# Store before weights, partial results after five sides, six early rows of h: one transformer layer step on one TensorE-bound core

## The chip, the cores and the metric

The kernel runs on one core of a Trainium2 chip. The metric is device time in microseconds (us) of one execution. The kernel before takes 2395.6 us in the median of three runs (2394.22 to 2397.26). One further execution was profiled; all rows below come from it. In the profile PE is TensorE (PEld its weight loads), DVE is VectorE, ACT is ScalarE, POOL is GpSimd, SP is SyncE; SP, ACT and POOL also issue the transfers (DMA) between the chip's main memory and the on-chip buffers.

## The reference, cut to what matters

One layer of a streaming encoder on 1024 prompt tokens and 32 sample tokens, with D_MODEL = 2048, all in float32:

```python
n = _rmsnorm(h, g_in)
z = n @ w_in                                   # 2048 x 6152: q, k, v, forget gate, ga, u, gs
att = _fox_attention(q, ..., k_all, v_all, ...)
ssm = _s5(u, ...)                              # state space scan, GELU, GLU with w_glu
mixed = concatenate([att * silu(ga), ssm * silu(gs)])
h = h + mixed @ w_out                          # 2048 x 2048
e = _rmsnorm(pe @ w_pe, g_pe)
h = h + e * sigmoid(h @ w_pg)                  # 2048 x 2048
y = _rmsnorm(h, g_final)
```

The two branches, the projections and the last norm are all computed; the keys, values, log forget gates and final states are outputs as well.

## The kernel before, in words

Every float32 product is done as three TensorE matmuls of rounded halves: an operand x is split into a high part (ACT casts it) and a low part (DVE subtracts the high part from x), and hi·hi, hi·lo and lo·hi are summed. The stages follow each other: the front (input projection, with the state-space branch in it), attention, side (the `w_pe` and `w_glu` products), mix (output projection), output (`w_pg` gate and final norm).

**Front and mix** are Strassen-Winograd products. A step p is one pair of column blocks, with seven products r = 0..6 of 24 matmuls each. The contraction is done in two halves: front steps 0 to 23 and mix steps 0 to 7 work on the first half, steps 24 to 47 and 8 to 15 on the second. At the change of halves, the seven stationary activation tiles ("sides", `t_act` and `m_t_act`) are exchanged: POOL reloads side s as soon as the last product that used it is done (`reload_side`), ACT makes its high part (`high_side`), DVE its low part (`low_side`, L1238 and L2890). In the first half a step's result is stored as a partial result (`cT<-zb`: L420 in the front, L2658 in the mix), and in the second half it is fetched back (`zb<-cT`, `load_part`, L667 and L2716) and put into the accumulators by ACT (`seed_x` L977 and L2795, then the second seed L982 and L2800).

SP carries the weights: each step needs two raw weight tiles of 512 KB (`load_w(p, 0)` and `load_w(p, 1)`, L415 and L2649). DVE first adds within them (the sums: L1297, L1301, L1306, L1309; L2918 and so on in the mix), ACT casts (L971, L2790), and DVE makes the low parts (L1316, L2936). DVE also adds products into the results (L1284, L1285, L1323, L1341, L1349; c22 is L1341, in the second half L1343; L2943, L2956, L2958 and L2964 in the mix). In each step the front's SP issues `load_w(p + 1, 1)`, then the store of the partial result, then `load_w(p + 2, 0)`; the mix's SP issues the store first and then both weight tiles.

In step 5 of the front the forget-gate weights are prepared by DVE behind its other work (`split_wf`, L1500 to L1506), and PE multiplies them in step 6 (L773).

**Side to mix.** The last output of the side stage is `mixT<-e_out`, issued by ACT (L2473); ACT ends the stage only when it has landed, and all engines wait for each other at a stage's end.

**Mix to output.** `hT` holds the layer's h in main memory, 16 rows of 128. The output product of a part (part 0: 512 tokens, part 1: 544) runs over w_pg column tiles; each tile needs all 16 rows of h, split. h comes back in groups of two rows through a ring of buffers `h_raw` with 4 groups; the first 4 groups are loaded during the mix, and their first 4 rows split behind the mix's last work (L2837 on ACT, L2976 on DVE), the rest in the output stage (L3206, L3270). At the turn from part 0 to part 1 DVE splits 12 rows of the next part, does the gate of part 0's last tile (L3279, L3284, L3287), splits the last 4 rows and then a weight tile (L140, L145). PE's transposes `y_ps` (L3158) of the gated tile stand inside part 1's first tile.

Within an engine, instructions run in program order, and what an engine needs from another it waits for with semaphores. The program has no scheduler: the loops in the code set the order.

Of the kernel before, what the change touches and what calls it, by code (L numbers as in the profile page):

```python
# [60 lines left out]
RING_H, EARLY_H = 4, 4  # L61
# [139 lines left out]
def stage_front(nc, d, G):  # L201
# [3 lines left out]
    with ExitStack() as ctx:  # L205
# [198 lines left out]
        def _(sp):  # L404
# [131 lines left out]
            for p in range(2 * NP):  # L536
# [88 lines left out]
        def _(pool):  # L625
# [279 lines left out]
        def _(act):  # L905
# [192 lines left out]
            def extra(p, j):  # L1098
# [96 lines left out]
        def _(dve):  # L1195
# [425 lines left out]
            def extra(p, j):  # L1621
# [702 lines left out]
def stage_side(nc, d, G):  # L2324

    with ExitStack() as ctx:
# [27 lines left out]
        gated_done, mix_stored = ([sem(f"{n}{b}") for b in range(2)] for n in ("gated_done", "glu_stored"))  # L2354
# [73 lines left out]
        def _(act):  # L2428
# [140 lines left out]
def stage_mix(nc, d, G):  # L2569


    with ExitStack() as ctx:  # L2572
# [66 lines left out]
        def _(sp):  # L2639
# [15 lines left out]
            for p in range(2 * NPM):  # L2655
# [9 lines left out]
                if p == last:  # L2665
                    for i in range(4):
                        sp.wait_ge(z_put[i], PUT + mix_count(NPM + RING_H - 1))
                    for g in range(RING_H):
# [7 lines left out]
        def _(pool):  # L2676
# [40 lines left out]

            for r in range(NRIDE):
                move_rides(r)
            for s in range(7):  # L2720
                reload_side(s)
                if s == 2:
                    load_part(NPM)
# [49 lines left out]
        def _(act):  # L2773
# [78 lines left out]
            for p in range(2 * NPM):  # L2852
                for j in range(7):
# [16 lines left out]
                    if j == 5 and NPM - 1 <= p < last:  # L2870
                        seed_x(p + 1)
                    high(7 * p + j + RING_W - 1)
                    for s in range(7):
                        if 7 * p + j == 7 * (NPM - 1) + s + 3:
# [3 lines left out]
            for k in range(EARLY_H):  # L2878
                high_h(k)

        @block.vector
        def _(dve):
# [112 lines left out]
            for p in range(2 * NPM):  # L2995
                for j in range(7):
                    if p == 0 and j < 3:
# [5 lines left out]
                    if j == 5:  # L3003
                        c22(p)
                    if j == 6:
# [7 lines left out]
                    for s in range(7):  # L3013
                        if 7 * p + j == 7 * (NPM - 1) + s + 4:
# [10 lines left out]
            for k in range(EARLY_H):  # L3025
                low_h(k)


def stage_output(nc, d, G):
# [11 lines left out]
    RING = 4  # L3041
    with ExitStack() as ctx:
# [6 lines left out]
        side, total, sig, h2 = ([sb(f"{n}{b}", [P, WM]) for b in range(2)]  # L3049
                                for n in ("side", "total", "gate_sig", "h2_"))  # L3050
        junk = nc.alloc_sbuf_tensor_at("junk", [P, YT, P], F32, offset=nc.sbuf_usable_end // 32 * 32 - 4 * YT * P)
# [136 lines left out]
        def _(act):  # L3188
# [12 lines left out]
            def high_h(part, k):  # L3201
                act.wait_ge(h_loaded[k // 2 % RING], 16 * (part * 2 + k // 2 // RING + 1))
# [6 lines left out]
                if k % 2 and (RING if part else RING + EARLY_H // 2) <= g < KD // 2:  # L3209
# [27 lines left out]
            for g in range(RING, RING + EARLY_H // 2):  # L3237
# [28 lines left out]
        def _(dve):  # L3266
# [64 lines left out]
            for part in range(2):  # L3331
# [61 lines left out]
def program(nc, d):  # L3393
# [3 lines left out]
    with ExitStack() as ctx:  # L3397
# [13 lines left out]
                          for i, n in enumerate("qkv")]  # L3411
# [10 lines left out]
                                            offset=(nc.sbuf_base + 31) // 32 * 32 + 256 + (3 + t) * 4 * KQ * HN) for t in range(2)]  # L3422
        G["m_loaded"] = [sem(f"m_w_loaded{s}") for s in range(3)]
        G["m_raw"] = [nc.alloc_sbuf_tensor_at(f"m_raw{s}", [P, KQ, 2 * P], F32, offset=top + s * 8 * KQ * P)
# [5 lines left out]
        def low(name, shape, dt=F32):  # L3430
# [9 lines left out]
                                             offset=top - 4 * RING_H * 2 * (T - 512)),  # L3440
# [27 lines left out]
```

## Time and profile before

| what | value |
|---|---|
| median of three runs | 2395.6 us |
| profiled execution, device time | 2394.27 us |
| its span in the profile | 2392.5 us |
| mean granted TensorE clock | 0.973 of full |
| PE busy | 2205.9 us (92%) |
| DVE busy | 1617.7 us (68%) |
| ACT busy | 906.0 us (38%) |
| POOL busy | 324.2 us (14%) |
| bytes moved | 424.80 MB, mean 178 GB/s |

The profiled execution lies 1.3 us under the median; 1.8 us of it lie outside the span. PE is idle for 186.6 us of the span, in pieces at the stage changes and the changes of halves. Times in the rows are us from the start of the span.

### The profile page before, as it was taken

What the parts mean: (1) busy time and instruction counts of PE and PEld (TensorE: products, weight loads), DVE (VectorE), ACT (ScalarE), POOL (GpSimd) and SP (SyncE); (2) the same over time, 40 slices, a digit from 0 to 9 for tenths busy, and PEclk for the clock granted to TensorE, in tenths of its full rate; (3) what the DMA queues carried; (4) which work ended last, traced back from release to release, by engine and by line L of the source; (5) the groups of instructions that cost most, each with busy time, mean ns of one, the idle gap of its engine ahead of it and who ended that gap; (6) DMA issues with size and microseconds to landing.
All of it is one profiled execution on the core that took longest, in us unless ns stands there. A gap on an engine that the chain in (4) does not pass through costs nothing. (4 is left out here: it accounts for less than half of the span.)

```text
span 2392.5 us, 44144 instructions
## 1 busy us (share of the span) xinstructions
PE 2205.9 (92%) x16355; PEld 2114.8 (88%) x16355; DVE 1617.7 (68%) x2941; ACT 906.0 (38%) x1843; POOL 324.2 (14%) x428
## 2 busy tenths in 40 slices
PE   3999999999899999999789978978989999999995
PEld 3999999999899999999778868978989987888995
DVE  6778766766787887886456646666657666666663
ACT  6542333333533333334366636224343331113112
POOL 0011000000111211111243410001111211111110
PEclk9999999999999999999899989989999999999997
DMA  8484444544757878785376655454556665346332
GB/s 244 146 258 111 142 138 123 151 135 127 272 185 207 230 218 237 217 224 165 129 238 202 199 178 188 130 198 148 189 206 233 217 221 159 111 126 202 100 100 97
DMA packets 362384, 424.80 MB, mean 178 GB/s; under 512 B 76064, under 2 KB 294792, under 8 KB 354336
## 3 DMA queue, kind: packets, MB, share of 16 engines
q1 hardware_dynamic: 306128, 266.62, 37.7%
q0 software_dynamic: 29504, 110.42, 13.5%
q10 hardware_dynamic: 26576, 45.40, 5.9%
q8 instruction: 112, 1.84, 0.3%
q14 instruction: 64, 0.52, 0.1%
HBM read 270.01 MB, written 143.68 MB: 173 GB/s over the span
## 5 line engine op out<-in xcount | busy, mean ns | idle before, releaser
L761 PE MATMUL acc<-t_act,w_hi 128*128 128x264 f32 x5376 | 889.1, 288 | 11.8 <-DVE zb L1323 3.8
L761 PEld LDWEIGHTS acc<-t_act,w_hi 128*128 128x128 f32 x5376 | 749.6, 189 | 18.6 <-issue 17.2
L761 PE MATMUL acc<-t_act,w_lo 128*128 128x264 f32 x2688 | 549.0, 286 | 0.0
L761 PEld LDWEIGHTS acc<-t_act,w_lo 128*128 128x128 f32 x2688 | 418.2, 189 | 0.0
L2763 PE MATMUL m_acc<-m_t_act,m_hi 128*128 128x264 f32 x1792 | 296.4, 288 | 19.9 <-ACT m_acc L2806 9.8
L1316 DVE TENSOR_TENSOR w_lo<-w_raw_f,w_hi 128x512 fp32r<-128x512 f32 x288 | 198.1, 688 | 145.2 <-ACT w_hi L971 144.6
L971 ACT CAST w_hi<-w_raw_f 128x512 fp32r<-128x512 f32 x288 | 177.9, 618 | 269.0 <-PE acc L761 247.4
L2763 PEld LDWEIGHTS m_acc<-m_t_act,m_hi 128*128 128x128 f32 x1792 | 252.9, 191 | 20.7 <-issue 19.7
L3170 PE MATMUL post_acc<-h_hi,w_post_hi 128*128 128x272 f32 (+1 forms) x768 | 211.2, 329 | 7.8 <-PEq L2572 4.3
L3170 PE MATMUL post_acc<-h_hi,w_post_lo 128*128 128x272 f32 (+1 forms) x768 | 208.2, 326 | 0.0
L3170 PE MATMUL post_acc<-h_lo,w_post_hi 128*128 128x272 f32 (+1 forms) x768 | 208.0, 325 | 0.0
L2763 PE MATMUL m_acc<-m_t_act,m_lo 128*128 128x264 f32 x896 | 184.6, 288 | 0.0
L3170 PEld LDWEIGHTS post_acc<-h_hi,w_post_hi 128*128 128x128 f32 x768 | 129.6, 190 | 21.0 <-DVE h_lo L3270 5.2
L2763 PEld LDWEIGHTS m_acc<-m_t_act,m_lo 128*128 128x128 f32 x896 | 141.0, 191 | 0.0
L3170 PEld LDWEIGHTS post_acc<-h_lo,w_post_hi 128*128 128x128 f32 x768 | 129.8, 190 | 10.6
L3170 PEld LDWEIGHTS post_acc<-h_hi,w_post_lo 128*128 128x128 f32 x768 | 129.1, 190 | 11.4
L2936 DVE TENSOR_TENSOR m_lo<-m_raw,m_hi 128x512 fp32r<-128x512 f32 x96 | 66.0, 689 | 53.3 <-ACT m_hi L2790 53.3
L3223 ACT ACTIVATE junk<-y_ps 128x128 f32<-128x128 f32 (+1 forms) x144 | 37.0, 274 | 170.6 <-PE y_ps L3158 170.6
L3284 DVE TENSOR_TENSOR h<-h,gate_sig 128x512 f32<-128x512 f32 (+1 forms) x32 | 22.7, 709 | 106.6 <-ACT gate_sig L3216 106.5
L652 POOL DMA_DIRECT2D zT<-zb x80 | 43.3, 542 | 343.0 <-DVE zb L1332 144.9
L3120 POOL TENSOR_TENSOR total<-h_hi,h_lo 128x512 f32 (+3 forms) x32 | 50.1, 1567 | 288.1 <-DVE h L3287 273.9
L2790 ACT CAST m_hi<-m_raw 128x512 fp32r<-128x512 f32 x96 | 59.2, 620 | 63.8 <-PE m_acc L2763 57.3
(435 smaller groups left out, 3633.9 us busy)
## 6 DMA issues: line engine op xcount, KB each, us to landing
w_raw_f<-in_w_in_dram SPq DMA_DIRECT2D x96, 512.0 KB, 4.1
w_raw<-in_w_pg_dram SPq DMA_DIRECT2D x64, 512.0 KB, 4.7
cT<-zb SPq DMA_DIRECT2D x24, 1056.0 KB, 4.6
zb<-cT POOLq DMA_DIRECT2D x96, 264.0 KB, 5.8
zT<-zb POOLq DMA_DIRECT2D x80, 264.0 KB, 3.7
m_raw<-in_w_out_dram SPq DMA_DIRECT2D x32, 512.0 KB, 5.8
eT<-e_out ACTq DMA_DIRECT2D x16, 528.0 KB, 3.1
cT<-m_zb SPq DMA_DIRECT2D x8, 1056.0 KB, 5.0
```

The source lines that it names most:

```text
L652: pool.dma_start(d["zT"][row:row + P, tok:tok + HN], zb[b][:, i]).then_inc(z_put[i], 16)
L761: mm = pe.matmul(out[:, c, 0:QN], w[:, k, :], t_act[:, SIDE[r], x, k, c * QN:(c + 1) * QN], start=(opens and k == 0 and m == 0), stop=(k = ...
L971: nc.scalar.copy(w_hi[n % RING_W][:], factor(p, r)).then_inc(hi_done, 1)
L1316: TT_(w_lo[n % RING_W][:], factor(n // 7, n % 7), w_hi[n % RING_W][:].bitcast(F32), ALU.subtract) \
L2763: mm = pe.matmul(out[:, c, 0:QN], w[:, k, :], t_act[:, MSIDE[r], x, k, c * QN:(c + 1) * QN], start=(opens and k == 0 and m == 0), stop=(k ...
L2790: nc.scalar.copy(w_hi[n % RING_W][:], factor(p, r)).then_inc(hi_done, 1)
L2936: TT_(w_lo[n % RING_W][:], factor(n // 7, n % 7), w_hi[n % RING_W][:].bitcast(F32), ALU.subtract) \
L3120: nc.gpsimd.tensor_tensor(total[b][:, 0:WIDTH[part]], row(hi, part, m).bitcast(F32), row(lo, part, m).bitcast(F32), ALU.add).then_inc(tota ...
L3170: mm = pe.matmul(acc[b][:, c, 0:width], w[:, k, :], a[:, k, start:start + width], start=(k == 0 and n == 0), stop=(k == KD - 1 and n == 2))
L3223: s = nc.scalar.activation(junk[0:rows, t], tr_ps[b][0:rows, t * P:(t + 1) * P], ACT.Square, accum_out=ssq[0:rows, t, bass.ds(m, 1)])
L3284: nc.vector.tensor_tensor(h2[b][:, 0:w], h2[b][:, 0:w], sig[b][:, 0:w], ALU.mult).then_inc(e_gated, 1)
```

## The change

Six edits, in the order of the program:

1. Front, SP: the store of a step's partial result is issued before `load_w(p + 1, 1)` in place of after it.
2. Front and mix, POOL: the first partial result is fetched back after five sides have been reloaded, in place of three.
3. Front and mix, ACT and DVE: `high_side` and `low_side` come one product slot later.
4. The ring of h has six groups in place of four, all six loaded in the mix. Six rows are split early in place of four, and DVE does this before c12 of the mix's last step. The last two groups are loaded at the start of the output stage.
5. Output, DVE: at the turn to part 1 the weight tile is split before the last four rows, and the gate of part 0's last tile comes after both.
6. Side: ACT no longer waits for the last stores of `mixT`; POOL and DVE wait for them in the mix before they read that data.

```diff
-                load_w(p + 1, 1)
                 if 1 <= p <= NP:
                     store_part(p - 1)
+                load_w(p + 1, 1)
...
             for s in range(7):
                 reload_side(s)
-                if s == 2:
+                if s == 4:
                     load_part(NP)
...
-                    if 7 * p + j == 7 * (NP - 1) + s + 3:
+                    if 7 * p + j == 7 * (NP - 1) + s + 4:
                         act.wait_ge(sides_moved[s], 16 * (RIDES + 1))
                         high_side(7 + s, s, t_act[:, SIDE[s], 1].bitcast(F32))
...
-                    if 7 * p + j == 7 * (NP - 1) + s + 4:
+                    if 7 * p + j == 7 * (NP - 1) + s + 5:
                         low_side(7 + s, s, t_act[:, SIDE[s], 1].bitcast(F32))
...
             for b in range(2):
                 act.wait_ge(e_stored[b], 16 * KD // 2)
-                act.wait_ge(mix_stored[b], 16 * KS // 2)
...
+            for b in range(2):
+                pool.wait_ge(G["glu_stored"][b], 16 * KS // 2)
             for r in range(NRIDE):
                 move_rides(r)
...
-RING_H, EARLY_H = 4, 4
+RING_H, EARLY_H = 6, 6
...
+                    if p == last and j == 6:
+                        for k in range(EARLY_H):
+                            low_h(k)
                     if j == 6:
                         c12(p)
...
             residual(last, 2)
             residual(last, 3)
-            for k in range(EARLY_H):
-                low_h(k)
...
-            for g in range(RING, RING + EARLY_H // 2):
+            for g in range(RING, GROUPS_H):
                 load_h(0, g)
...
                 if part == 0:
                     for k in range(KD - 4):
                         low_h(1, k)
-                gate(part, KD - 1, 1, KD // 2 - 1)
-                if part == 0:
+                    W.split_tile(dve, nc, KD + 1, 1, True)
                     for k in range(KD - 4, KD):
                         low_h(1, k)
-                    W.split_tile(dve, nc, KD + 1, 1, True)
+                gate(part, KD - 1, 1, KD // 2 - 1)
                 fill(part, KD - 1, 1)
```

What moves on the engines. On SP, one step of the front (`w_raw_f` are weights, `cT<-zb` the store, `wf_rawa` the forget-gate weights, so this is step 5):

```order
-L415 DMA w_raw_f<-in_w_in_dram 128x4x256
-L420 DMA cT<-zb 128x2112
-L415 DMA w_raw_f<-in_w_in_dram 128x4x256
+L420 DMA cT<-zb 128x2112
+L415 DMA w_raw_f<-in_w_in_dram 128x4x256 x2
 L487 DMA wf_rawa<-in_w_in_dram 128x16x8
```

The store of 1056 KB now stands ahead of both weight tiles. The same happens in each of the steps 1 to 24.

On DVE, the change of halves in the front, before the change (`t_act` is the low part of a side, `w_lo` of a weight):

```order
 L1488 TENSOR_TENSOR d_diag<-d_bc_93,ident 16x64
 L1491 TENSOR_TENSOR kern<-kern,d_diag 16x4x16
-L1238 TENSOR_TENSOR t_act<-t_act 128x2112
 L1341 TENSOR_TENSOR zb<-zb,acc 128x528
 L1301 TENSOR_TENSOR w_raw_f<-w_raw_f 128x4x128
...
 L1297 TENSOR_TENSOR w_raw_f<-w_raw_f 128x4x128
 L1316 TENSOR_TENSOR w_lo<-w_raw_f,w_hi 128x512
+L1238 TENSOR_TENSOR t_act<-t_act 128x2112
 L1343 TENSOR_TENSOR u_out<-acc,zb 128x66x8
```

The low part of side 0 no longer stands ahead of step 23's c22 (L1341); every side's low part moves one slot back, and that of side 6 now stands ahead of step 24's c22 (L1343).

On POOL, the same place (`t_act<-tS` are sides, `zb<-cT` partial results):

```order
-L641 DMA t_act<-tS 128x2112 x3
-L667 DMA zb<-cT 128x528 x4
-L641 DMA t_act<-tS 128x2112 x4
+L641 DMA t_act<-tS 128x2112 x5
+L667 DMA zb<-cT 128x528 x4
+L641 DMA t_act<-tS 128x2112 x2
```

Two transfers of a side pass the four pieces of the partial result.

## Rows read from the trace of the kernel before

**Rows 1.** The page, section 1: busy time of each engine.

```profile
PE 2205.9 (92%) x16355; PEld 2114.8 (88%) x16355; DVE 1617.7 (68%) x2941; ACT 906.0 (38%) x1843; POOL 324.2 (14%) x428
```

**Rows 2.** Windows (stretch, length, busy us per engine, PEclk, DMA share, GB/s).

```profile
214.00:216.00 2.00, 2.00 (x11) 2.00 (x11) 1.83 (x10) 0.00 (x0) 0.00 (x0) 0.50 0.89 376
```

**Rows 3.** Timeline of SP, step 5 of the front (start, duration, engine, line, operation).

```profile
187.93 0.39 SPq L415 DMA_DIRECT2D w_raw_f<-in_w_in_dram  x1
192.00 0.35 SPq L420 DMA_DIRECT2D cT<-zb  x1
```

**Rows 4.** Timeline of DVE and PE there ([idle before <-releaser]).

```profile
194.26 0.69 DVE L1297 TENSOR_TENSOR w_raw_f<-w_raw_f 128x512 f32<-128x512 f32 x1
...
213.74 5.69 PE L773 MATMUL oth<-t_act,wf_twoa 128*128 128x264 f32 x32 [4.68 <-DVE wf_twoa L1506]
```

**Rows 5.** Timeline of SP and DVE, one step of the mix.

```profile
1666.43 0.34 SPq L2658 DMA_DIRECT2D cT<-m_zb  x1
...
1674.28 0.69 DVE L2918 TENSOR_TENSOR m_raw<-m_raw,m_raw 128x512 f32<-128x512 f32 x1 [3.40 <-DMA m_raw<-in_w_out_dram]
```

**Rows 6.** The page, section 6: KB each, median us from issue to landing.

```profile
w_raw_f<-in_w_in_dram SPq DMA_DIRECT2D x96, 512.0 KB, 4.1
```

**Rows 7.** Timeline of SP and DVE, front's change of halves.

```profile
603.32 0.33 SPq L420 DMA_DIRECT2D cT<-zb  x1
...
607.17 0.69 DVE L1297 TENSOR_TENSOR w_raw_f<-w_raw_f 128x512 f32<-128x512 f32 x1
...
621.62 2.35 DVE L1238 TENSOR_TENSOR t_act<-t_act 128x2112 fp32r<-128x2112 f32 x1
...
645.30 1.12 DVE L1343 TENSOR_TENSOR u_out<-acc,zb 128x528 f32<-128x528 f32 x1
```

**Rows 8.** Timeline of PE there: first matmuls after a wait.

```profile
615.10 0.72 PE L761 MATMUL acc<-t_act,w_hi 128*128 128x264 f32 x4 [0.93 <-DVE zb L1341]
620.58 1.22 PE L761 MATMUL acc<-t_act,w_hi 128*128 128x264 f32 x4 [2.32 <-ACT acc L977]
628.11 1.22 PE L761 MATMUL acc<-t_act,w_hi 128*128 128x264 f32 x4 [3.04 <-ACT acc L982]
```

**Rows 9.** Timeline of SP, DVE, ACT and PE, mix's change of halves.

```profile
1769.65 3.89 SPq L2649 DMA_DIRECT2D m_raw<-in_w_out_dram  x2
...
1782.51 0.69 DVE L2918 TENSOR_TENSOR m_raw<-m_raw,m_raw 128x512 f32<-128x512 f32 x1 [9.36 <-DMA m_raw<-in_w_out_dram]
...
1783.62 0.60 ACT L2795 COPY m_acc<-m_zb 128x528 f32<-128x528 f32 x1 [5.08 <-DMA m_zb<-cT]
...
1786.84 1.22 PE L2763 MATMUL m_acc<-m_t_act,m_hi 128*128 128x264 f32 x4 [6.76 <-DVE m_zb L2956]
```

**Rows 10.** Timeline of DVE and ACT, from side to mix.

```profile
1592.24 2.06 DVE L2542 TENSOR_TENSOR e_out<-sig,gs 128x1056 f32<-128x1056 f32 x1
...
1598.17 1.95 ACT L2777 CAST m_t_act<-m_b 128x2112 fp32r<-128x2112 f32 x1 [7.32 <-PEq L2326]
```

**Rows 11.** Timeline of DVE, POOL and PE, from mix to output.

```profile
1960.37 2.49 DVE L2976 TENSOR_TENSOR h_lo<-h_raw,h_hi 128x512 fp32r<-128x512 f32 x4
...
1960.75 0.54 POOL L2704 DMA_DIRECT2D hT<-m_zb  x1 [1.79 <-DVE m_zb L2971]
...
1963.41 0.77 PE L3170 MATMUL post_acc<-h_hi,w_post_hi 128*128 128x512 f32 x1 [4.33 <-PEq L2572]
...
1975.87 0.50 PE L3170 MATMUL post_acc<-h_hi,w_post_hi 128*128 128x512 f32 x1 [2.51 <-DVE h_lo L3270]
```

**Rows 12.** Timeline of DVE and PE, the turn to part 1.

```profile
2163.37 2.62 DVE L3270 TENSOR_TENSOR h_lo<-h_raw,h_hi 128x544 fp32r<-128x544 f32 x4
...
2167.11 2.35 DVE L145 TENSOR_TENSOR w_post_lo<-w_raw,w_post_hi 128x1024 fp32r<-128x1024 f32 x2
...
2163.55 0.63 PE L3158 MATMUL y_ps<-ident,h 128*128 128x128 f32 x4 [2.25 <-issue]
2179.47 0.77 PE L3158 MATMUL y_ps<-ident,h 128*128 128x128 f32 x5 [3.26 <-issue]
```

More of the change, by code:

```diff
@@ L2353, in stage_side @@
         summed = [sem(f"e_summed{b}") for b in range(2)]
-        gated_done, mix_stored = ([sem(f"{n}{b}") for b in range(2)] for n in ("gated_done", "glu_stored"))
+        gated_done, mix_stored = [sem(f"gated_done{b}") for b in range(2)], G["glu_stored"]
         block = ctx.enter_context(nc.Block(no_gpsimd_drain=True))
@@ L2667, in _ @@
                         sp.wait_ge(z_put[i], PUT + mix_count(NPM + RING_H - 1))
+                    sp.wait_ge(lo_done, 7 * last)
                     for g in range(RING_H):
@@ L2721, in _ @@
                 reload_side(s)
-                if s == 2:
+                if s == 4:
                     load_part(NPM)
@@ L2996, in _ @@
                 for j in range(7):
+                    if p == 0 and j == 0:
+                        for b in range(2):
+                            dve.wait_ge(G["glu_stored"][b], 16 * KS // 2)
                     if p == 0 and j < 3:
@@ L3004, in _ @@
                         c22(p)
+                    if p == last and j == 6:
+                        for k in range(EARLY_H):
+                            low_h(k)
                     if j == 6:
@@ L3013, in _ @@
                     for s in range(7):
-                        if 7 * p + j == 7 * (NPM - 1) + s + 4:
+                        if 7 * p + j == 7 * (NPM - 1) + s + 5:
                             low_side(7 + s, s)
@@ L3024, in _ @@
             residual(last, 3)
-            for k in range(EARLY_H):
-                low_h(k)
 def stage_output(nc, d, G):
@@ L3040, in stage_output @@
     YT = len(ROWS[1])
-    RING = 4
+    RING = RING_H
+    GROUPS_H = KD // 2
     with ExitStack() as ctx:
@@ L3048, in stage_output @@
         y_tok, g_bc = sb("y_tok", [P, YT, D_MODEL]), sb("g_bc", [P, D_MODEL])
-        side, total, sig, h2 = ([sb(f"{n}{b}", [P, WM]) for b in range(2)]
-                                for n in ("side", "total", "gate_sig", "h2_"))
-        junk = nc.alloc_sbuf_tensor_at("junk", [P, YT, P], F32, offset=nc.sbuf_usable_end // 32 * 32 - 4 * YT * P)
+        side, total, sig = ([sb(f"{n}{b}", [P, WM]) for b in range(2)] for n in ("side", "total", "gate_sig"))
+        top = nc.sbuf_usable_end // 32 * 32 - 4 * YT * P
+        h2 = [nc.alloc_sbuf_tensor_at(f"h2_{b}", [P, WM], F32, offset=top - (b + 1) * 4 * WM) for b in range(2)]
+        junk = nc.alloc_sbuf_tensor_at("junk", [P, YT, P], F32, offset=top)
         g_pe = sb("g_pe_s", [P, KD])
@@ L3201, in high_h @@
             def high_h(part, k):
-                act.wait_ge(h_loaded[k // 2 % RING], 16 * (part * 2 + k // 2 // RING + 1))
+                g = k // 2
+                act.wait_ge(h_loaded[g % RING], 16 * (part * len(range(g % RING, GROUPS_H, RING)) + g // RING + 1))
                 if part == 1:
@@ L3208, in high_h @@
                 g = k // 2 - 1 + RING
-                if k % 2 and (RING if part else RING + EARLY_H // 2) <= g < KD // 2:
+                if part and k % 2 and RING <= g < KD // 2:
                     load_h(part, g)
@@ L3422, in program @@
                                             offset=(nc.sbuf_base + 31) // 32 * 32 + 256 + (3 + t) * 4 * KQ * HN) for t in range(2)]
+        G["glu_stored"] = [sem(f"glu_stored{b}") for b in range(2)]
         G["m_loaded"] = [sem(f"m_w_loaded{s}") for s in range(3)]
-        G["m_raw"] = [nc.alloc_sbuf_tensor_at(f"m_raw{s}", [P, KQ, 2 * P], F32, offset=top + s * 8 * KQ * P)
+        G["m_raw"] = [nc.alloc_sbuf_tensor_at(f"m_raw{s}", [P, KQ, 2 * P], F32, offset=top + (s + 1) % 3 * 8 * KQ * P)
                       for s in range(3)]
@@ L3439, in program @@
             "h_raw": nc.alloc_sbuf_tensor_at("h_raw", [P, RING_H, 2, T - 512], F32,
[L3440 removed]
+                                             offset=top + 8 * KQ * P - 4 * RING_H * 2 * (T - 512)),
             "h_loaded": [sem(f"h_loaded{s}") for s in range(RING_H)],
```

4 lines of the change are left out of this document (2 added, 2 removed).

## The prediction

> **What bounds the kernel now.** I read the busy times first: PE works 92% of the span, DVE 68% [rows 1]. So TensorE's work is the floor, and the change adds and removes no matmul. It can only win or lose in the 186 us in which PE is idle, and these lie at the stage changes and the changes of halves. I then read PE's timeline at each place that an edit touches, for the gap and its releaser, and the timelines of the releasers, back to the transfer or the DVE queue that came last. The reader is to see six places. In the front's step 5, PE waits 4.68 us for the forget-gate weights, the last thing in a DVE queue [rows 4]. At the front's change of halves there are gaps of 0.93, 2.32 and 3.04 us, the last two for accumulators that ACT seeds [rows 8]. At the mix's change of halves there is one of 6.76 us for c22, behind a DVE stall of 9.36 us for a weight tile [rows 9]. From side to mix all engines wait for ACT's last store [rows 10]. From mix to output PE waits 4.33 us at the stage's start and then for late rows of h [rows 11]. At the turn to part 1 it waits 2.25 and 3.26 us [rows 12]. After a gap the matmuls are slow too: the granted clock is 0.50 in the 2 us behind step 5's gap [rows 2], which is the 1.2 GHz level, and the first four matmuls behind a gap take 1.22 us in place of 0.72 [rows 8].
>
> **Side's last store (edit 6): -2.7 us.** DVE ends its last operation at 1594.30, and ACT, which issues the store then, resumes only at 1598.17 after 7.32 us of waiting at the stage's end [rows 10]. Without the wait the stage begins about 1 us behind DVE's end, at 1595.3: 2.9 us earlier. The new waits stand on POOL and DVE; ahead of them nothing of the mix is late, and by the time that DVE reaches its own (behind its first part of a side, at least 2.35 us, the length of such an operation [rows 7]) the store has had some 4 us. The store now shares the transfer engines with the mix's first blocks. I count 0.2 us for that; the bounds are -3.2 and -1.
>
> **Ring of six, six early rows (edit 4): -5 us.** Before, DVE's four early rows end at 1962.86, after POOL's last issue at 1961.29, so they set the stage's end [rows 11]. They move ahead of c12, into time in which DVE waits for PE. The stage's end then falls to about 1961.5 (POOL, and 0.2 to 0.4 us that c12 comes later behind six rows), a gain of 1.4 us. In the first tile, the 2.51 us that PE waits at 1975.87 for rows of h is a wait for late groups [rows 11]. Six rows are ready now, and the last two groups are asked for at the stage's start, not behind ACT's casts. That wait goes, and with it the shorter ones and some of the slow start, 3.6 us in all by my estimate. If the two groups are as late as before, because they wait for the last `hT` store and share the engines with w_pg, only 1.4 us are won. The bounds are -1.4 and -6.5.
>
> **Gate behind the split (edit 5): +1.4 us.** The gate ended just ahead of 2163.37 and released `y_ps` at 2163.55. Now four rows (2.62 us) and a weight tile (from 2165.99 to 2169.46, 3.5 us) stand ahead of it [rows 12]. PE, ready 2.25 us before 2163.55, waits up to 6.1 us longer; with the ring of six the rows ahead come some 1.7 us sooner, so 4.4 us. Between the two `y_ps` PE has 12.66 us of work (2179.47 - 3.26 - 2163.55). It would reach the second at 2163.55 + 4.4 + 12.66 = 2180.6 in place of being released at 2179.47, so 3.26 us of the loss come back and +1.2 remain; with 6.1 us it is +2.8. I take +1.4, bounds 0 and +2.8.
>
> **Store ahead of the weights, step 5 of the front (edit 1): +4.6 us.** The tile `load_w(6, 1)` was issued at 187.93; now it follows the store at 192.00 [rows 3]. Its first sum stood at 194.26, with no wait [rows 4]. The mix has this order already: there the store is issued at 1666.43 and the sum starts at 1674.28 after a wait of 3.40 us, 7.85 us behind the store [rows 5]; six steps of the mix show 6.56 to 7.85. That puts step 5's sum at 198.6 to 199.9, 4.3 to 5.6 us late. DVE has no pause worth naming from there to the forget-gate weights, for which PE waits already [rows 4], so PE loses the whole delay. If the tile needed only the front's median of 4.1 us [rows 6], it would land at 192.4 + 4.1 = 196.5, and the loss is 2.2 us. The front moves less than the mix at that time, so I take 4.6; the bounds are 2 and 5.6.
>
> The Trainium skill ("DMA: Bandwidth & Descriptors", section "Queues, rings and completion order") says that a transfer engine takes the descriptors of one issuer's ring in order and turns between rings. By that rule the tile starts behind the whole store, which is the 4.6 us case; without it the tile would land on its own time, the 2.2 us case. The 7.85 us of the mix against the 4.1 us of the front's tiles speak for the rule.
>
> In steps 1 to 4 and 6 to 22 the same swap makes the sum late by up to the same few microseconds. What hides it is that c22, behind it on DVE, still waits for PE, and that DVE is free for a third of the span [rows 1]. In the mix the same order makes DVE wait 3.40 us [rows 5] without a gap on PE. So I count 0; were that cover gone in the front, each of the 21 steps would cost up to 1.5 us, over 30 us in all, which I hold for very unlikely.
>
> **Front's change of halves (edits 1 to 3): +3.5 us.** Three things meet. First, the tile behind the store. Issued at 603.7 instead of ahead of the store, with the sides running as in the mix, it lands as there, 12.86 us behind its issue (1769.65 to 1782.51 [rows 9]), at 616.6. Its sum ran at 607.17 [rows 7]. Then c22 ends near 618.5 and PE's wait of 0.93 us at 615.10 becomes 4.4; the next product, released at 620.58 [rows 8], starts at 621.6, 1 us late. Second, side 0's low part no longer runs in DVE's free time; it joins a queue that is busy without a pause from 621.62 to 646.42 [rows 7], and seven sides in place of six stand ahead of step 24's c22: +2.35 us. Third, sides 3 and 4 come ahead of the partial results, and the 3.04 us at 628.11, behind a side that came late, may go; but the queue of DVE sets the end of this step, so that gain is mostly given back. With the tile at 616.6 I get 1 + 2.35, and 3.5 in round numbers. If the tile takes only 4.1 us [rows 6], it is 2.35 - 3.04 = -0.7; if sides 3 and 4 hold it back by another 2 us, +5. Bounds -0.7 and +5.
>
> **Mix's change of halves (edits 2, 3): +1.7 us.** The store is ahead already, so the stall of 9.36 us stays. Side 0's low part (2.35 us, the same size as in the front [rows 7]) moves behind c22, so that PE's gap of 6.76 us [rows 9] shrinks by as much. But DVE has the same work after it, and the seed at 1783.62, which waited 5.08 us for its partial result [rows 9], comes later by what two sides of 528 KB take ahead of it: 0 to the 4.1 us of a tile of that size [rows 6]. What c22 wins is won again by no one, since the next product needs that seed. Bounds -0.5 and +4; I take 1.7, below the middle, because POOL waits for the partial result's store to land anyway.
>
> **Sum.** -2.7 - 5 + 1.4 + 4.6 + 3.5 + 1.7 = +3.5 us. On the profiled execution that is 2394.27 + 3.5 = 2397.8 us; its own time lies 1.3 us under the median, so the median to expect is 2399 us. The bounds added up give -8.9 and +15, but they will not all fall on one side; the rivals take those that hang together.
>
> **The rivals.**
>
> Faster: transfers are not the limit. A tile behind the store lands in its own 4.1 us, and the partial results are not held up. Then step 5 costs 2.2, the front's change of halves -0.7, the mix's -0.5, and with -2.7, -5 and +0.7 the sum is -6: 2389.6 us. For it: the medians of rows 6, and that PE waits for nothing in the mix's steady steps. Against it: the 7.85 us of rows 5 and the 12.86 us of rows 9 are the same order, measured. Chance 0.27.
>
> Slower: the weight tile starves behind the store while the sides run. The place is the two changes of halves; it decides from the point where the tile lands later than 616.6 in the front, because from there DVE's queue of 24.8 us begins later and every microsecond is PE's. Two more sides in the air at that time make it +5, the seed in the mix +4, step 5 +5.6; with -2.7, -5 and +1.4 the sum is +8.3: 2404 us. For it: the 9.36 us stall of rows 9 with only three sides ahead. Against it: the store itself starts without a tile ahead of it and may land sooner. Chance 0.27.
>
> The change doesn't do what it says at the output: the two late groups of h wait for the last `hT` store and land as late as before, so that the ring of six gives 1.4 and not 5 us. The other terms as in the forecast, the sum is +7.1: 2402.7 us. For it: PE's wait at 1975.87 stands in a stretch where w_pg loads run too; against it: the groups are asked for several microseconds sooner. Chance 0.11.
>
> **How the numbers follow.** A measurement of this kernel can tell about 0.2% from no change, 4.8 us. The forecast, 2399 us with its own range of 2395 to 2402, has a chance of 0.35; most of it (0.29) lies within 4.8 us and 0.06 above. The faster rival gives 0.25 faster and 0.02 within; the slower one 0.22 slower and 0.05 within; the last one 0.07 slower and 0.04 within. Together: faster 0.25, within 0.40, slower 0.35. The range of 8 in 10 reaches from 2387, past the faster rival and near the lower bound of the sum (2386.7), to 2408, past the slower one and 2.6 us short of the upper bound.
>
> **What would show it.** In the profile after: ACT's first cast of the mix within 1.5 us of DVE's last operation of side; PE's first gate matmul near 1961.9 plus what came before, and no wait over 1 us for h in the first tile; `y_ps` at the turn behind a wait of 6 to 7 us and the second without one; step 5's first sum behind a wait of 4 to 5 us for `w_raw_f`, and PE's wait for the forget-gate weights shifted by the same; a wait of 9 us for `w_raw_f` at the front's change of halves. I am wrong if that stall is under 3 us (then the faster rival holds), or if PE waits for c22 in the front's plain steps.

## The result and the profile after

The changed kernel is slower: 2411.24 us in the median of six runs against 2395.32, ratio 1.0064 with a 95% interval of 1.0052 to 1.0076, so 12 to 18 us. One of its runs took 2977.73 us, far from all others; without it, as in the ratio, the median of the other five is 2409.68 us, and differences from the changed kernel below are taken from that. The profiled execution has a span of 2408.0 us, 15.5 more than before. PE's busy time differs by 3.5 us only (2209.4 against 2205.9): it waits more.

To see where, I took the first matmul of the same product in both traces and subtracted the starts. The table gives what each stretch added, for the changed kernel and for two of the runs below that undo one edit each (all in us, against the profiled execution of before):

| stretch | changed | edit 1 undone | edit 2 undone | predicted |
|---|---|---|---|---|
| front, steps 0 to 6 | +7.6 | +1.3 | +8.5 | +4.6 |
| front's change of halves | +4.8 | +5.5 | -0.2 | +3.5 |
| rest of front, attention, side to the end of its DVE work | +1.8 | | | 0 |
| side to mix, with mix step 0 | -2.9 | | | -2.7 |
| mix's change of halves | +4.5 | +4.7 | -0.5 | +1.7 |
| output | -0.3 | 0.0 | +0.8 | -3.6 |
| sum (span) | +15.5 | +7.5 | +4.4 | +3.5 |

The front's steps and both changes of halves lose, as forecast, and more than forecast; output won nothing. One trace stands for each kernel here, so small entries are to be read with care: by step 7 of the front the ten traces without edit 1 stand 0.0 to 2.1 us behind the kernel before, the five with edit 1 as it is 6.6 to 9.1 us; and the stretch from the rest of the front to the end of side's DVE work, in which no edit changes anything, lies between -1.0 and +2.5 us in all of them.

Step 5 of the front, timelines of SP, DVE and PE of the changed kernel:

```profile
194.83 0.35 SPq L420 DMA_DIRECT2D cT<-zb  x1
195.27 2.30 SPq L415 DMA_DIRECT2D w_raw_f<-in_w_in_dram  x2
...
174.83 0.69 DVE L1297 TENSOR_TENSOR w_raw_f<-w_raw_f 128x512 f32<-128x512 f32 x1 [4.99 <-DMA w_raw_f<-in_w_in_dram]
...
202.29 0.69 DVE L1297 TENSOR_TENSOR w_raw_f<-w_raw_f 128x512 f32<-128x512 f32 x1 [5.12 <-DMA w_raw_f<-in_w_in_dram]
...
176.88 0.72 PE L761 MATMUL acc<-t_act,w_hi 128*128 128x264 f32 x4 [1.30 <-DVE zb L1341]
...
204.34 1.22 PE L761 MATMUL acc<-t_act,w_hi 128*128 128x264 f32 x4 [5.11 <-DVE zb L1341]
```

Against [rows 3, 4] the tile follows the store at once, and the sum waits 5.12 us for it, 7.46 us behind the store. That was the forecast. But step 4 has the same wait (4.99 us, at 174.83), and PE stands for c22 in both steps, 1.30 and 5.11 us. Step 5 loses 6.7 us by this; the wait for the forget-gate weights behind it is even a little shorter than before (3.94 us in place of 4.68). And PE restarts slowly, which windows (columns as in [rows 2]) show as a granted clock of 0.50 and then 0.66, so the 1.2 GHz level for most of 4 us:

```profile
204.00:206.00 2.00, 1.66 (x7) 1.69 (x8) 2.00 (x5) 0.62 (x1) 0.00 (x0) 0.50 0.33 37
206.00:208.00 2.00, 2.00 (x14) 2.00 (x13) 2.00 (x12) 0.00 (x0) 0.00 (x0) 0.66 0.00 0
```

The front's change of halves, POOL, ACT, DVE and PE:

```profile
619.39 0.53 POOL L641 DMA_DIRECT2D t_act<-tS  x1 [2.41 <-PE acc L761]
619.91 2.13 POOL L667 DMA_DIRECT2D zb<-cT  x4
...
630.07 0.60 ACT L977 COPY acc<-zb 128x528 f32<-128x528 f32 x1 [11.15 <-DMA zb<-cT]
...
628.92 0.69 DVE L1297 TENSOR_TENSOR w_raw_f<-w_raw_f 128x512 f32<-128x512 f32 x1 [14.06 <-DMA w_raw_f<-in_w_in_dram]
...
631.35 1.22 PE L761 MATMUL acc<-t_act,w_hi 128*128 128x264 f32 x4 [9.57 <-DVE zb L1341]
...
658.96 0.72 PE L761 MATMUL acc<-t_act,w_hi 128*128 128x264 f32 x4 [2.16 <-DVE u_out L1343]
```

Two things are late now. The weight tile's sum waits 14.06 us (forecast: 9), and the seed comes 10.16 us behind the issue of the partial result. PE's gap for c22, 0.93 us in [rows 8], is 9.57. The waits of 2.32 and 3.04 us in [rows 8] are gone; the 2.16 us at 658.96 are for step 24's c22. For comparison, the partial result and its seed in the kernel before, where the seed comes 3.75 us behind the issue:

```profile
616.08 2.13 POOL L667 DMA_DIRECT2D zb<-cT  x4 [9.64 <-DMA cT<-zb]
...
619.83 0.60 ACT L977 COPY acc<-zb 128x528 f32<-128x528 f32 x1 [4.43 <-DMA zb<-cT]
```

The mix's change of halves, against [rows 9]:

```profile
1780.87 3.89 SPq L2648 DMA_DIRECT2D m_raw<-in_w_out_dram  x2
...
1789.42 2.14 POOL L2716 DMA_DIRECT2D m_zb<-cT  x4
...
1797.49 0.69 DVE L2921 TENSOR_TENSOR m_raw<-m_raw,m_raw 128x512 f32<-128x512 f32 x1 [13.12 <-DMA m_raw<-in_w_out_dram]
...
1800.10 0.60 ACT L2797 COPY m_acc<-m_zb 128x528 f32<-128x528 f32 x1 [11.65 <-DMA m_zb<-cT]
...
1799.55 1.22 PE L2765 MATMUL m_acc<-m_t_act,m_hi 128*128 128x264 f32 x4 [8.25 <-DVE m_zb L2959]
```

The same pair: the tile, whose place behind the store did not change here, waits 13.12 us in place of 9.36, and the seed is 10.68 us behind its issue, in place of 6.26 (issued at 1777.36 before, seeded at 1783.62).

From side to mix, and the output's start and turn, against [rows 10 to 12]:

```profile
1606.37 2.05 DVE L2541 TENSOR_TENSOR e_out<-sig,gs 128x1056 f32<-128x1056 f32 x1
...
1609.97 1.95 ACT L2779 CAST m_t_act<-m_b 128x2112 fp32r<-128x2112 f32 x1 [4.98 <-PEq L2326]
...
1978.00 0.47 PE L3179 MATMUL post_acc<-h_hi,w_post_hi 128*128 128x512 f32 x1 [3.17 <-PEq L2571]
1987.90 0.51 PE L3179 MATMUL post_acc<-h_hi,w_post_hi 128*128 128x512 f32 x1 [2.54 <-DVE h_lo L3280]
...
2178.82 0.74 DVE L3289 SCALAR_TENSOR_TENSOR h<-side,g_pe_s,e_rstd 128x512 f32<-128x512 f32 x1
...
2181.11 1.09 PE L3167 MATMUL y_ps<-ident,h 128*128 128x128 f32 x4 [6.22 <-issue]
```

ACT begins the mix 1.55 us behind DVE's end (3.87 before); the forecast was about 1. The output starts behind a wait of 3.17 us in place of 4.33, yet 2.54 us in the first tile remain (2.51 before). At the turn there is one wait of 6.22 us with slow matmuls (1.09 in place of 0.63) for the two of 2.25 and 3.26.

### The profile page after: what moved, and what is told of

Read it like the earlier page. It is cut to its first block and busy times, and to the rows that moved or that the text cites. A ratio compares the mean times of both kernels' runs of the same rounds, so it can differ in the third digit from the quotient of the medians.

```text
span 2408.0 us, 44145 instructions
## 1 busy us (share of the span) xinstructions
PE 2209.4 (92%) x16355; PEld 2117.5 (88%) x16355; DVE 1616.2 (67%) x2941; ACT 905.8 (38%) x1843; POOL 325.1 (13%) x428
```

## The experiments

The runs of the kernel before on the same chips gave medians of 2393.6 to 2394.6 us. Differences below are between medians unless a trace is named.

**Undo edit 1.**

```diff
-                if 1 <= p <= NP:
-                    store_part(p - 1)
                 load_w(p + 1, 1)
+                if 1 <= p <= NP:
+                    store_part(p - 1)
```

> The changed kernel with edit 1 alone undone: in the front the tile load_w(p + 1, 1) is issued ahead of the store again. Theory 1 (the tile behind the store is the loss in the whole front): step 5 gives back its 7.6 us, and at the front's change of halves DVE's stall of 14.06 us for w_raw_f goes, so that most of the 4.75 us there come back too; about 2400 us, 11 to 12 under the changed kernel. Theory 2 (at the change of halves the five sides ahead of the partial results and the later split are the loss): step 5 gives back 7.6 us and the 4.75 us stay; about 2403.5 us.

Measured: 2402.61 us, ratio 1.0035 (1.0022 to 1.0049), 7.1 us under the changed kernel. Steps 0 to 6 give back 6.3 us in the trace, and the change of halves nothing: 5.5 us lost there. Theory 2. The tile is on time here, and the partial result is not:

```profile
615.19 2.13 POOL L667 DMA_DIRECT2D zb<-cT  x4 [1.57 <-DMA cT<-zb]
...
625.04 0.60 ACT L977 COPY acc<-zb 128x528 f32<-128x528 f32 x1 [12.41 <-DMA zb<-cT]
...
626.23 0.69 DVE L1316 TENSOR_TENSOR w_lo<-w_raw_f,w_hi 128x512 fp32r<-128x512 f32 x1 [12.33 <-ACT w_hi L971]
...
629.29 1.22 PE L761 MATMUL acc<-t_act,w_hi 128*128 128x264 f32 x4 [10.86 <-DVE t_act L1238]
```

The partial result is issued 0.9 us earlier than in the kernel before (616.08), although this trace is 1.3 us late by step 7, and it is seeded 9.85 us behind that; before it was 3.75. ACT's next cast stands behind the seed, DVE waits 12.33 us for that cast, and PE for the low part of a side behind it on DVE.

**Same issue time, other place in the queue.**

```diff
                 if 1 <= p <= NP:
-                    store_part(p - 1)
+                    sp.wait_ge(added, p)
                 load_w(p + 1, 1)
+                if 1 <= p <= NP:
+                    store_part(p - 1)
```

> The changed kernel, but SP waits for the store's data first, then issues the tile load_w(p + 1, 1), then the store. The tile is issued as late as in the changed kernel, only ahead of the store in SP's queue. Theory 1a (the place in the queue counts): the tile lands some 4 us behind its issue, step 5's wait for w_raw_f falls from 5.12 to about 2 us and the 14.06 us at the change of halves to 5 us or less; 2402 to 2405 us. Theory 1b (the late issue counts, since all transfers share the same engines): the waits stay at about 5 and 12 to 14 us; 2410 to 2412 us.

Measured: 2405.63 us, 1.0042 (1.0029 to 1.0056), 4.0 us back and 0.6 above theory 1a's range. Step 5's wait for the tile falls from 5.12 to 2.45 us and steps 0 to 6 lose 4.9 in place of 7.6; at the change of halves the wait falls from 14.06 to 3.64. So the place behind the store in SP's queue is a good part of the delay, theory 1a, and the late issue the rest: of the 6.3 us that edit 1 costs by step 6, 2.75 are the place and 3.55 the lateness. And again the change of halves loses 6.0 us although the tile is waited for 10 us less.

**Undo edit 2.**

```diff
-                if s == 4:
+                if s == 2:
                     load_part(NP)
```

(and the same for `load_part(NPM)`)

> The changed kernel with edit 2 alone undone, in front and mix: the partial results are fetched after three sides. Theory A (the partial results behind sides 3 and 4 hold up the seed): at the mix's change of halves the seed, 16.5 us behind the one of before, of which 11.2 are older, comes some 4 us earlier and most of the 4.5 us lost there come back; in the front 1 to 2 us; 2405 to 2407 us. Theory B (the tile behind the store and the later split are the loss): 2410 to 2411 us, and c22's wait stays the same.

Measured: 2398.69 us, 1.0019 (1.0010 to 1.0028), 11.0 us back; theory A, and far more than it said. Both changes of halves are even with the kernel before. The front's, in this run:

```profile
619.71 2.13 POOL L667 DMA_DIRECT2D zb<-cT  x4 [4.77 <-DMA cT<-zb]
...
625.86 0.60 ACT L977 COPY acc<-zb 128x528 f32<-128x528 f32 x1 [6.03 <-DMA zb<-cT]
...
624.88 0.69 DVE L1297 TENSOR_TENSOR w_raw_f<-w_raw_f 128x512 f32<-128x512 f32 x1 [9.13 <-DMA w_raw_f<-in_w_in_dram]
...
627.31 1.22 PE L761 MATMUL acc<-t_act,w_hi 128*128 128x264 f32 x4 [4.63 <-DVE zb L1341]
```

The partial result is issued 0.2 us earlier than in the changed kernel and seeded 4.2 us earlier; the tile, issued by SP, comes 4.0 us earlier too. The tile's wait of 9.13 us is as I forecast it from the mix, and it costs nothing net: c22 is waited for 3.7 us longer than in [rows 8], but the waits of 2.32 and 3.04 us behind it there are gone.

**Undo edit 3.**

```diff
-                    if 7 * p + j == 7 * (NP - 1) + s + 4:
+                    if 7 * p + j == 7 * (NP - 1) + s + 3:
```

(and `low_side` from `+ 5` to `+ 4`, both in front and mix)

> The changed kernel with edit 3 alone undone, in front and mix: the sides are split in the slots of before. Theory A (side 0's low part of 2.35 us now stands in DVE's busy queue): 2 us or so come back at each change of halves, 2406 to 2408 us. Theory B (DVE stalls for the tile anyway, so that side 0's part, ahead of c22 or behind it, stands behind the same stall): nothing in the front, where c22 even comes 2.35 us later behind the stall, and nothing in the mix; 2410 to 2413 us.

Measured: 2408.68 us, 1.0058 (1.0045 to 1.0072), between the two ranges; in the trace both changes of halves still lose (5.3 and 5.8 us). Theory B in the traces: beside late tiles and seeds, the slot does not matter.

**Four sides ahead.**

```diff
-                if s == 4:
+                if s == 3:
```

> The changed kernel with the partial results fetched after four sides, in place of five (changed) or three (before). If each side ahead of them in POOL's queue costs its own time, the seed comes about half of the way back and 4 to 7 us of the 12.5 that three sides gave return: 2404 to 2407 us. If it is a threshold (the fifth side only is issued late enough to matter, or only the fourth), the time is near 2399 or near 2411 us.

Measured: 2405.41 us, 1.0045 (1.0031 to 1.0058), in the range of "each side costs", but not evenly: in the trace the front's change of halves still loses 4.6 us and the mix's 3.4. The front's seed is 7.83 us behind its issue, between 6.15 with three sides and 10.16 with five. But it is the tile that PE stands for here, 8.27 us for c22: the seed comes no later than before, counted from the losses up to step 7, and the tile 12.8 us later than its sum of before.

```profile
627.97 0.69 DVE L1297 TENSOR_TENSOR w_raw_f<-w_raw_f 128x512 f32<-128x512 f32 x1 [12.76 <-DMA w_raw_f<-in_w_in_dram]
...
627.44 0.60 ACT L977 COPY acc<-zb 128x528 f32<-128x528 f32 x1 [8.16 <-DMA zb<-cT]
```

**Edits alone, on the kernel before.** Edit 1 alone:

> The kernel before with edit 1 alone. Theory 1 (the prediction's: the tile behind the store also costs 3.5 us or so at the front's change of halves): step 5 costs 6 and the change of halves 3 to 4, 2402 to 2404 us. Theory 2 (a late tile at the change of halves only fills a time in which the partial result is waited for anyway; step 5 is all): 2399 to 2401 us.

Measured: 2403.26 us, 1.0039 (1.0025 to 1.0052). The time lies in theory 1's range, but the trace is theory 2: steps 0 to 6 lose 9.1 us and the change of halves nothing (-0.1). Edit 2 alone:

> The kernel before with edit 2 alone. Theory 1 (the partial results land late behind sides 3 and 4 whatever the split's slot and the tile's place): 4 to 6 us at each change of halves, 2402 to 2406 us. Theory 2 (it is the three edits together that hurt: with the split in the old slots the later seed costs little): under 5 us in all, 2395 to 2398 us.

Measured: 2404.92 us, 1.0043 (1.0029 to 1.0056): theory 1; 4.8 us at the front's change of halves, 4.0 at the mix's. Edit 6 alone:

> The kernel before with edit 6 alone. Theory 1 (the mix starts as much earlier as ACT waited, 2.3 us in the changed kernel's trace, and nothing gives it back): 2391 to 2392 us. Theory 2 (the store's 1 MB, now beside the mix's first blocks, makes these land later and takes it back): 2393 to 2394 us.

Measured: 2391.68 us, 0.9990 (0.9981 to 0.9999), 2.3 us won: theory 1.

**Sides 3 and 4 by another queue.** On the kernel before with edit 2 alone:

```diff
+                    if p == NP - 1 and j == 4:
+                        for r in (3, 4):
+                            act.wait_ge(sides_moved[r], 16 * RIDES)
+                            act.wait_ge(prod_done, 7 * (NP - 1) + r + 1)
+                            act.dma_start(t_act[:, SIDE[r], 1].bitcast(F32), d["tS"][r]).then_inc({3: sin_done, 4: cos_done}[r], 16)
...
```

(the same in the mix; POOL leaves these two out, and fetches the partial result behind sides 0 to 2)

> The kernel before with edit 2 alone, but sides 3 and 4 are fetched by ACT's queue and not by POOL's, at about the same time: they move the same bytes in the same stretch, and only do not stand ahead of the partial results in POOL's queue. Theory 1 (the place in the queue is what holds the partial results up): the seed comes some 4 us behind its issue as in the kernel before, where edit 2 alone needs 8, and each change of halves is within 1.5 us of the kernel before; 2394 to 2397 us. Theory 2 (all queues share the same engines; two more sides at this time hold up the partial results and the tile wherever they stand): 4 to 5 us at each change of halves, as with edit 2 alone; 2402 to 2405 us.

Measured: 2400.49 us, 1.0035 (1.0022 to 1.0049), between the two. The changes of halves lose 4.1 and 3.2 us where edit 2 alone loses 4.8 and 4.0. The front's seed:

```profile
610.24 0.34 ACTq L1190 DMA_DIRECT2D t_act<-tS  x1
...
612.94 0.34 ACTq L1190 DMA_DIRECT2D t_act<-tS  x1
...
624.00 0.60 ACT L979 COPY acc<-zb 128x528 f32<-128x528 f32 x1 [6.27 <-DMA zb<-cT]
```

POOL issued the partial result at 617.11, so 6.89 us, against 7.98 with all in POOL's queue and 3.75 before. In the mix it is otherwise:

```profile
1782.33 2.13 POOL L2724 DMA_DIRECT2D m_zb<-cT  x4 [5.01 <-DMA cT<-m_zb]
...
1788.75 0.60 ACT L2804 COPY m_acc<-m_zb 128x528 f32<-128x528 f32 x1 [4.14 <-DMA m_zb<-cT]
...
1790.76 0.69 DVE L2933 TENSOR_TENSOR m_raw<-m_raw,m_raw 128x512 f32<-128x512 f32 x1 [12.63 <-DMA m_raw<-in_w_out_dram]
...
1795.09 1.22 PE L2772 MATMUL m_acc<-m_t_act,m_hi 128*128 128x264 f32 x4 [10.04 <-DVE m_zb L2971]
```

The seed is 6.42 us behind its issue, as before (6.26) and not as with edit 2 alone (10.70); but the tile on SP's queue still waits 12.63 us, and PE stands 10.04 us for c22 behind it, 3.28 more than in [rows 9]. So the mix's loss here is the tile's. Theory 2 holds for what is lost: in these traces four fifths of it stay when the sides stand in no one's way but on the engines (between the medians it is 6.7 of 11.0 us). Theory 1 holds for the mix's seed. The Trainium skill ("DMA: Bandwidth & Descriptors", section "Issuing engines are not separate DMA queues") says that transfers of all issuers run on the same 16 engines and interleave; the 4.1 and 3.2 us agree.

**What the traces say together.** How late the tile's sum and the first seed are, against the kernel before and counted from what each trace had lost by step 7 of its stage, and what the change of halves loses (us):

| run | front: tile | seed | loss | mix: tile | seed | loss |
|---|---|---|---|---|---|---|
| edit 1 alone | 9.2 | -2.3 | -0.1 | -0.3 | -0.1 | -0.3 |
| changed, edit 2 undone | 9.2 | -2.5 | -0.2 | -0.1 | 0.2 | -0.5 |
| changed, four sides | 12.8 | -0.4 | 4.6 | 4.0 | 2.2 | 3.4 |
| changed | 14.2 | 2.6 | 4.8 | 3.8 | 5.3 | 4.5 |
| changed, edit 1 undone | 0.0 | 3.9 | 5.5 | 5.3 | 5.1 | 4.7 |
| edit 2 alone | 0.0 | 3.5 | 4.8 | 4.0 | 5.3 | 4.0 |
| edit 2, sides by ACT | 0.0 | 2.6 | 4.1 | 3.3 | 0.1 | 3.2 |

In the front a tile 9.2 us late costs nothing, one 12.8 us late costs 4.6 with the seed on time, and with the tile on time a late seed costs as much. In the changed kernel both are late, so taking away one of them alone wins nothing there. In the mix every late row has a late tile, and PE's first wait there is for c22 in all of them.

**Without edits 1 and 2.** The kernel with edits 3 to 6:

> The changed kernel with edits 1 and 2 undone; edits 3 to 6 stay. From the two single runs: step 5 gives back 6.3 us and the two changes of halves 4.9 and 5.0, so 2411 - 16 = 2395 us if nothing else is left; the stage trace of the changed kernel has 2.3 us won from side to mix and near 0 for output. Theory 1 (edits 1 and 2 hold the whole loss, edit 6 wins): 2392 to 2394 us, the front and the mix within 1 us of the kernel before. Theory 2 (the later split costs too, because side 0's low part stands in the busy queue once the tile and the partial result are on time): 2 us more at each change of halves, 2396 to 2398 us.

Measured: 2392.99 us, 0.9996 (0.9987 to 1.0005), no change that can be told. The time is theory 1's; in the trace the front's change of halves loses 2.8 us, which is theory 2's, and the mix's none. PE's first wait in the front is now 6.61 us for a side's low part (L1238). Then edit 5 undone too, and ACT's order changed:

```diff
-            for g in range(RING, GROUPS_H):
-                load_h(0, g)
-            for k in range(EARLY_H, KD):
+            for k in range(EARLY_H, 2 * RING):
+                high_h(0, k)
+            for g in range(RING, GROUPS_H):
+                load_h(0, g)
+            for k in range(2 * RING, KD):
                 high_h(0, k)
```

> As the run with edits 1 and 2 undone, and in the output stage ACT casts h's rows 6 to 11 before it issues the last two group loads, and the gate stands ahead of the last four rows again (edit 5 undone). Theory 1 (ACT's wait for the last hT store, in front of casts that could run, took back the gain of the early rows, and edit 5 costs 1 to 2 us): 2 to 4 us faster than that run. Theory 2 (the landing of the last two groups sets the first tile, whatever ACT does before, and the gate's place only moves a wait): within 1 us of that run.

Measured: 2391.27 us, 0.9989 (0.9980 to 0.9998); 1.7 us better, between the two. Then the mix's tile ahead of its store:

> As the run before, and in the mix the tile load_w(p + 1, 1) is issued ahead of the store, as the front of the kernel before does it. Theory 1 (the store ahead of the tile costs the mix's change of halves what it would cost the front's): DVE's stall of 9.3 us for the tile there goes to under 2, and 2 to 4 us are won. Theory 2 (the partial result's landing sets that place, the tile only fills the same wait): the stall goes, but less than 1 us is won.

Measured: 2391.08 us, 0.9990 (0.9981 to 0.9999). Theory 2: DVE's wait for the tile (9.06 us) is gone from the trace and nothing is won. PE's wait only moved from step 7's last product (4.18 us, for c22, in the run before) to step 8's first:

```profile
1787.93 1.22 PE L2765 MATMUL m_acc<-m_t_act,m_hi 128*128 128x264 f32 x4 [6.37 <-DVE m_t_act L2893]
```

This is the low part of a side, whose cast on ACT stands behind the seed.

**Edits 4 and 6 alone**, with that order of ACT:

> Edits 4 and 6 alone of the change (the ring of six with six early rows, with ACT's casts ahead of the last two group loads; no wait for side's last store); edits 1, 2, 3 and 5 undone. In the run with edit 3 still in, the front's change of halves was 2.4 us behind the kernel before. Theory 1 (the later split costs these 2 us once the tile and the partial results are on time, because side 0's low part stands in DVE's busy queue): front even with before, 2388.5 to 2390 us. Theory 2 (the 2.4 us are scatter of the transfers): 2391 to 2392 us.

Measured: 2388.84 us, 0.9973 (0.9962 to 0.9984). Faster than both kernels, by 5.1 us against before. Against the run with edit 3 in, 2.4 us, though the two intervals touch (0.9980 to 0.9998 there); the front's change of halves is even with before (-0.4 in the trace). Theory 1: the three traces with edit 3, and without edits 1 and 2, lose 1.1 to 2.8 us there, the four with none of the three -0.7 to +0.8. With edit 5 put back:

> Edits 4 (with ACT's casts ahead of the last two group loads), 5 and 6; that is the fastest run so far with edit 5 put back. Theory 1 (the gate behind the split costs what the prediction has): 1 to 2.5 us slower than that run, 2390 to 2391.5 us. Theory 2 (the second wait's end gives all of it back): 2388.5 to 2389.5 us.

Measured: 2391.86 us, 0.9994 (0.9985 to 1.0003): edit 5 costs 3.0 us, theory 1 and more. With the loads ahead of the casts again, as the change has it:

> Edits 4 as it was and 6: the fastest run so far with the last two group loads ahead of ACT's casts again. Theory 1 (ACT's wait for the last hT store, ahead of casts that could run, took back part of the ring's gain): 1 to 3 us slower than that run, 2390 to 2392 us. Theory 2 (the landing of these two groups sets the first tile, and an earlier issue helps as much as the late casts cost): within 1 us of that run.

Measured: 2388.77 us, 0.9981 (0.9972 to 0.9990): theory 2, the order of loads and casts does not show in the time. In the trace PE's wait for the last rows in the first tile is 1.27 us here, against 2.63 in the run with the casts ahead; of the other seven runs with the loads ahead one has 1.20, and six 2.49 or more. The wait, and then the turn in this run, and behind it in the run with edit 5:

```profile
1972.83 0.50 PE L3179 MATMUL post_acc<-h_hi,w_post_hi 128*128 128x512 f32 x1 [1.27 <-DVE h_lo L3280]
...
2158.60 0.63 PE L3167 MATMUL y_ps<-ident,h 128*128 128x128 f32 x4 [0.20 <-issue]
2174.51 1.30 PE L3167 MATMUL y_ps<-ident,h 128*128 128x128 f32 x5 [3.27 <-issue]
```

```profile
2164.26 1.09 PE L3167 MATMUL y_ps<-ident,h 128*128 128x128 f32 x4 [6.22 <-issue]
```

The ring of six alone takes the first wait from 2.25 us [rows 12] to 0.20; edit 5 makes one wait of 6.22 us out of 0.20 and 3.27, 2.75 more.

## Why the prediction was wrong

The direction of the sum was right (3.5 us slower), the size was not, and the measured 2411 us lies above the range and above the slower rival. Three steps failed: that nothing is lost in the front's steps 1 to 4 and that step 5 loses at the forget-gate weights; the size of the sides in the mix's term; and the first tile of output in the ring's term. By its steps:

- **Side's last store, -2.7:** right. -2.3 in the trace, -2.3 alone.
- **Ring of six, -5:** too large. In the changed kernel's trace the stage's start came 1.2 us earlier (forecast 1.4), and the first tile won 0.9 us (forecast 3.6). Edits 4 and 6 together win 5.1 us, of which edit 6 is 2.3, so 2.8. I took the wait for the last rows for late asking; it is late landing. ACT asks for the last two groups from 1980.80 on, and its casts of the last of them wait again:

```profile
1990.65 1.14 ACT L3216 CAST h_hi<-h_raw 128x512 fp32r<-128x512 f32 x2 [2.69 <-DMA h_raw<-hT]
```

The last rival had this ("land as late as before") and I gave it 0.11. Why PE's wait is 1.2 to 1.3 us in two of the runs and 2.2 us or more in the other ten with the ring, no run shows.

- **Gate behind the split, +1.4:** as a part of the sum about right: the turn's waits go from 5.51 to 6.22 us, and the changed kernel's trace loses 1.7 us there. But I had counted the ring's help in this term (4.4 us in place of 6.1) and so mistook what edit 5 costs. The ring alone makes the first wait 0.20 us; on top of that, edit 5 costs 3.0 us.
- **Store ahead of the weights, +4.6 (2 to 5.6):** 7.6 in the changed kernel, 6.3 of it taken back by undoing edit 1, 9.1 alone; the trace of before is itself about a microsecond ahead of most others here. The stall itself was right: 5.12 us against 4.3 to 5.6. What failed is the sentence that nothing is lost in steps 1 to 4: step 4 stalls 4.99 us and hands on 1.9 us (1.30 us of it a gap on PE), and the loss of step 5 falls on c22, where the gap of 5.11 us brings a restart at 1.2 GHz. I followed only DVE's queue to the forget-gate weights and did not ask which product needs c22 on the way. PE waiting for c22 in a plain step was among my own signs of being wrong.
- **Front's change of halves, +3.5:** 4.8, near in size by accident. I let a tile 9.4 us late cost 1 us and put the rest on side 0's low part. A tile 9.2 us late cost nothing, alone or with edits 3 to 6. What costs is edit 2, which I had as a gain mostly given back: it makes the tile 14.2 us late and the seed 2.6, and either is enough. Side 0's later low part shows only once edits 1 and 2 are undone, at 1.1 to 2.8 us.
- **Mix's change of halves, +1.7 (-0.5 to +4):** 4.5. The term for two sides ahead of the partial result was mis-sized, and at the root by a misreading: a side has 1056 KB, not 528, and its own row in the trace of before has 10.4 us from issue to landing in the front, where I took at most the 4.1 us of a weight tile:

```profile
t_act<-tS POOLq DMA_DIRECT2D x7, 1056.0 KB, 10.4
```

The seed went from 6.26 to 10.68 us behind its issue, 4.4 us, and the wait for the weight tile from 9.36 to 13.12. I priced the sides as a delay of the transfer that follows them in POOL's queue. They also delay the tile on SP's queue, and c22 behind that tile is what PE waits for first.

- **Steps 6 to 22 at 0:** right for steps 7 to 22, where no trace moved; step 6 gives back 1.0 us of step 5's loss.

Of the rivals, the faster one (transfers are not the limit) is out. The slower one named the right places and, for the front, a point of decision that fits: a tile later than 616.6, which is 9.4 us behind its sum of before, and it was 14.2 us late. It lacked the second way, by the seed, and its 4 us for the mix came from the seed alone. Shown: edit 2 causes the loss at both changes of halves (undone, alone, and by another queue), edit 1 that up to step 6 of the front. Not settled: how much of the mix's loss the seed would cause by itself, since no run has it late with the tile on time; why one more side delays the front's tile from 9.2 to 12.8 us; and the 3 us by which the rest of the front, attention and side differ from run to run.

## What to carry to other kernels

At these two places several transfers are in flight at once, and one that was brought forward was paid for by others, on its own queue and on another. Before moving a transfer, list what is in flight there with the sizes and landing times of the page, and ask which of them PE needs first. A stall of a shared engine must be followed to each consumer on its way, not only to the last one. Where two late transfers hold up the same place, as here, undoing one of them alone can win nothing, and that does not clear it. And edits to one place are to be costed in sequence, each on the trace that the one before it leaves: here edits 4 and 6 alone make the kernel 0.27% faster (0.9973, 0.9962 to 0.9984), and the other four take it away.

## What the runs showed of the hardware

- The same tile of 512 KB from main memory was waited for not at all, 3.64, 9.13 or 14.06 us at the same place, by its place in SP's queue and by what POOL fetched at that time.
- Four pieces of 264 KB were seeded 3.1 to 6.2 us behind their issue in the front with three sides of 1056 KB ahead of them, 7.8 with four, and 7.4 to 10.2 with five. In the mix it was 5.3 to 6.9, 8.3 and 10.5 to 10.8 us. Moving two sides to another queue gave back 1.1 of 4.2 us in the front and all but 0.2 of 4.4 us in the mix, where the tile on a third queue stayed 3.3 us late.
- A DVE wait of 9 us for the mix's weight tile could be removed without any gain: PE's wait moved on to the next product, which stands behind the seed.
